# The second network's down product in units of seven products, with row sums on GpSimd

## The chip, the cores and the metric

The kernel runs on one core of a Trainium2 chip. The metric is the device time of one execution in microseconds, and the time of a kernel is the median of its runs. The engines are called PE (TensorE, with PEld for its weight loads), DVE (VectorE), ACT (ScalarE), POOL (GpSimd) and SP (SyncE, which here issues the large transfers).

## The reference, cut to what matters

Two transformer blocks follow one another on one sequence of 256 tokens of width 2048, all in float32. The second block ends with a gated network whose down product is changed here:

```python
def conv_ffn(h, w_up, conv_w, w_down):
    u = h @ w_up                                   # (256, 2048) @ (2048, 11264)
    ... causal depthwise convolution of width 3 over the tokens ...
    gate, val = jnp.split(c, 2, axis=-1)
    return (jax.nn.silu(gate) * val) @ w_down      # (256, 5632) @ (5632, 2048)

x = x + rms_norm(conv_ffn(h, ffn_w_up[i], ffn_conv[i], ffn_w_down[i]), norm_g[i, 3])
```

The norm divides each token's row by the root of its mean square and multiplies it with a gain for each column. Its result is added to the residual x and returned.

## The kernel before, in words

Every large product is done as float32 in two parts. A tile of weights, called a chunk (128 x 2 x 512 values: two blocks k of 128 rows and 512 columns), is fetched by SP into `raw`. ACT rounds it to a shorter format (`cast`, tile `whi`), DVE takes the difference to the original (`subtract`, tile `wlo`), and PE multiplies three times: high rows by high weights, high by low, low by high. The rows (the activations, transposed) are split in the same manner: `Hh` and `Hl` hold the hidden activations of the second network, 44 blocks k of 128 by 256 tokens.

A plain chunk takes two k by two halves of the tokens by three, which is 12 matmuls of 512 columns. They accumulate in two PSUM banks for each group of 512 output columns. The down product of the second network (stage `dn2`) has 4 groups of 22 chunks, 88 in all, one group after the other. Group i has the banks 2i and 2i + 1.

The order of all of this is one list, `weight_steps`. Each engine's program goes through it and does its own part of each step. ACT and DVE run up to three steps ahead of PE (`ahead`), as far as the ring of `whi` and `wlo` tiles lets them: there are three slots, and a fourth one (`WX`) in the first network. `side_steps` gives work that is put at a step; an engine does it after the casts or subtractions that are ahead of that step. `empties` does the same for finished groups. Waits are on semaphores counted in program order, so an instruction that waits also holds what stands behind it on its engine. SP fetches in the list's order and waits for a free slot of `raw`.

The first network's down product (stage `dn`) already has nine **units of seven products**. A unit takes the two chunks of one pair p of blocks k in two neighbouring groups of columns. This is a 2 x 2 by 2 x 2 block product: rows (token half by k) times columns (k by group). The Winograd form of Strassen's scheme needs seven products for it in place of eight. It needs sums of the weights, which DVE makes (`wsum`: one instruction of 1024 elements and two of 512, on tiles `RX` and `TD`), and sums of the rows, which DVE makes too (`xa`, `xc`). In the list a unit has four steps:

- `c`: two products with the original weights,
- `f`: two products with changed weights,
- `b`: one product with the sum in `TD`,
- `h`: two products with changed weights.

Plain chunks (`w`) stand between them. `stream_unit` issues the 21 matmuls. Four of the seven products (the kinds) are wanted by more than one output tile, so they have banks 4 to 7 of their own and are added to the outputs by DVE afterwards (`fold0` to `fold3`, after ACT's `fsnap` has copied one bank).

At the end of the kernel `stream_last` does the last three chunks by token half: all of them for the first 128 tokens, then for the others. For each half, ACT squares the last group straight out of PSUM, DVE makes the mean, multiplies the last group by the gain `GB` and waits for POOL, which takes the power -0.5. DVE then updates x in four instructions, and SP writes each one out.

Of the kernel before, what the change touches and what calls it, by code (L numbers as in the profile page):

```python
# [12 lines left out]
ALU = mybir.AluOpType  # L13
# [24 lines left out]
EXP = (4, 8, 12, 16, 5, 9)  # L38

# [9 lines left out]
def weight_chunks():  # L49
# [44 lines left out]
    product("dn2", "ffn_w_down_2", n4, FT)  # L94
# [36 lines left out]
def down_chunks(chunks):  # L131

    return {(row[1], row[2] // 2): t for t, row in enumerate(chunks) if row[0] == "dn"}


def down_units(chunks):

    at = down_chunks(chunks)
    return {at[2 * h + z, p]: (3 * h + q, z) for h in range(2) for q, p in enumerate(DU[h]) for z in range(2)}
# [30 lines left out]
def weight_steps(chunks):  # L170
# [21 lines left out]
    return rows + [("w", t) for t in range(IN2, END)]  # L192
# [67 lines left out]
def side_steps(chunks):  # L260
# [133 lines left out]
    for g in range(2 * NF):  # L394
        for f in range(4):
            for j in range(3 if g % 2 == 0 else 5):
                put(FF2 + 8 * g + 8 + 2 * f + j, "conv%d" % j, 4 * g + f)
    return at
# [64 lines left out]
def build(nc, A):  # L463
    ctx = ExitStack()
    with ctx:
# [86 lines left out]
        MG2 = at("MG2", rT, 0, [2, D])  # L552
        NAT = at("NAT", rN, 0, [2, 1024])
# [82 lines left out]
        forms = form_order(chunks)  # L636
        form_rank = {p: r for r, (p, _) in enumerate(forms)}
# [35 lines left out]
        def unit_steps(n):  # L673
            i, p = (0, DU[0][n]) if n < 3 else (2, DU[1][n - 3])
            return {kind: step_of[kind, down[i + (kind == "f"), p]] for kind in "cfbh"}
# [7 lines left out]
        def whole(u):  # L683

            kind, t = work[u]
            if kind == "b":
                return TD[:, units[t][0] % 2, :]
# [111 lines left out]
        def sync_program(eng):  # L799
            sp = Seat(eng)  # L800

            def fetch(t):
                _, _, k0, a, n, name, c = chunks[t]
                if t in units and raw_before[t] < DN:
                    sp.wait_ge(s_mm, upto[DN])
                elif raw_before[t] is not None:
# [40 lines left out]
        def gpsimd_program(eng):  # L847
# [11 lines left out]

            eng.memset(MHALF[:, :], -0.5).then_inc(s_mhalf, 1)  # L860
# [46 lines left out]
            row_rstd(7)  # L907
            for t in range(2):
# [4 lines left out]
        def scalar_program(eng):  # L913
# [44 lines left out]
            def empty(g):  # L958
# [73 lines left out]
                elif st in ("post", "dn2"):  # L1032
                    for t in range(2):
# [4 lines left out]
                        square(b[t][:, :], 6 if st == "post" else 8, 4 * t + i)  # L1038
# [5 lines left out]
            def side(name, i, t):  # L1044
# [128 lines left out]
                elif name == "fsnap":  # L1173
# [3 lines left out]
                    copy(SD[:, 0, :], bank[4][:, :]).then_inc(s_snap, 1)  # L1177
                elif name == "sqb":
# [97 lines left out]
        def vector_program(eng):  # L1276
# [50 lines left out]
            def empty(g):  # L1327
# [92 lines left out]
                elif st == "dn2":  # L1420
                    if i < 3:
                        ve.wait_ge(l_g3, 16)
                        for t in range(2):
                            cs_ = slice(512 * i, 512 * (i + 1))
                            ve.wait_ge(s_sq, SQ[7] + 2 * i + t + 1)
                            eng.tensor_tensor(MG2[:, t, cs_], b[t][:, :], GB[:, cs_], ALU.mult).then_inc(s_emptyV, 1)
# [62 lines left out]
            def side(name, i, t):  # L1489
# [177 lines left out]
                elif name == "wsum":  # L1667

                    h, p = (0, DU[0][i]) if i < 3 else (2, DU[1][i - 3])
                    for z in range(2):  # L1670
                        n = down[h + z, p]
# [4 lines left out]
                    ve.wait_ge(s_wsum, 3 * i + 1)  # L1676
                    if i >= 2:
# [3 lines left out]
                    eng.tensor_tensor(TD[:, i % 2, :], z[:, 3, :], z[:, 0, :], ALU.subtract).then_inc(s_wsum, 1)  # L1681
                    ve.wait_ge(s_wsum, 3 * i + 2)
                    eng.tensor_tensor(z[:, 1, :], z[:, 1, :], TD[:, i % 2, :], ALU.subtract).then_inc(s_wsum, 1)
# [17 lines left out]
                elif name == "fold3":  # L1701
# [4 lines left out]
                    eng.tensor_tensor(xs, xs, SD[:, 2, :], ALU.add).then_inc(s_fold, 1)  # L1706
                elif name == "between":
# [161 lines left out]
            b = [bank[z] for z in banks["dn2", 3]]  # L1869
            for t in range(2):  # L1870
# [5 lines left out]
                eng.tensor_tensor(MG2[:, t, 1536:D], b[t][:, :], GB[:, 1536:D], ALU.mult).then_inc(s_emptyV, 1)  # L1876
                ve.wait_ge(s_rs, 9 + t)
                for c in range(4):
                    xs = slice(512 * c, 512 * (c + 1))
                    ve.wait_ge(*emptied_at(("dn2", c), t))  # L1880
                    eng.scalar_tensor_tensor(out=X[:, t, xs], in0=MG2[:, t, xs], scalar=rs_7[:, t:t + 1],
                                             in1=X[:, t, xs], op0=ALU.mult, op1=ALU.add).then_inc(s_fin, 1)


        def tensor_program(eng):
# [35 lines left out]
            def begins(g, half):  # L1921
# [4 lines left out]
                if g[0] == "dn2":  # L1926
                    pe.wait_ge(s_cv0, 84 if g[1] < 2 else 88)
# [9 lines left out]
            def stream_unit(u):  # L1937
# [3 lines left out]
                h, k = n // 3 > 0, chunks[t][2]  # L1941
                left, right = ("dn", 2 * h), ("dn", 2 * h + 1)
                opens, ends = n in (0, 3), n in (2, NU - 1)
                hi, lo = two(hi_at(u)), two(lo_at(u))

                def rows(k, half):
                    return tuple(z[:, half * P:(half + 1) * P] for z in hidden(k))

                def sums_of_rows(z):
                    e = ex_at(n)  # L1950
# [4 lines left out]
                if kind == "c":  # L1955
                    products = ((None, 4, rows(k, 0)), (left, 0, rows(k + 1, 0)))
                elif kind == "b":
                    products = ((None, 5, sums_of_rows(2)),)
                elif kind == "f":
                    products = ((None, 6, sums_of_rows(3)), (right, 0, sums_of_rows(4)))  # L1960
# [445 lines left out]
```

## Time and profile before

| what | value |
|---|---|
| median of 3 runs | 2325.8 us (2325.62 to 2333.89) |
| span of the profiled execution | 2323.6 us, 2.2 us below the median |
| PE busy | 2303.2 us, 99% |
| VectorE busy | 1689.3 us, 73% |
| ScalarE busy | 1255.4 us, 54% |
| GpSimd busy | 20.3 us, 1% |
| moved by DMA | 439.28 MB, 189 GB/s on average |

The profile is one execution. The span goes from its first to its last instruction; the time of the same execution outside the profiler is not given beside it, so the median of the runs stands for it, and the 2.2 us between the two is what lies around the span. A busy PE need not be a PE at its peak, because matmuls overlap and their ends are modelled: the distance from one start to the next counts, not the recorded duration.

### The profile page before, as it was taken

What the parts mean: (1) busy time and instruction counts of PE and PEld (TensorE: products, weight loads), DVE (VectorE), ACT (ScalarE), POOL (GpSimd) and SP (SyncE); (2) the same over time, 40 slices, a digit from 0 to 9 for tenths busy, and PEclk for the clock granted to TensorE, in tenths of its full rate; (3) what the DMA queues carried; (4) which work ended last, traced back from release to release, by engine and by line L of the source; (5) the groups of instructions that cost most, each with busy time, mean ns of one, the idle gap of its engine ahead of it and who ended that gap; (6) DMA issues with size and microseconds to landing.
All of it is one profiled execution on the core that took longest, in us unless ns stands there. A gap on an engine that the chain in (4) does not pass through costs nothing.

```text
span 2323.6 us, 29041 instructions
## 1 busy us (share of the span) xinstructions
PE 2303.2 (99%) x11236; PEld 1941.5 (84%) x11236; DVE 1689.3 (73%) x2356; ACT 1255.4 (54%) x1854; POOL 20.3 (1%) x34
## 2 busy tenths in 40 slices
PE   9999999999999999999999999999999999999998
PEld 7888888888788888888888888888888888888887
DVE  6445565666788888887878777967888888885444
ACT  7445464555555555555655567866444444444443
POOL 1000000000000000000000000000000000000000
PEclk9999999999999999999999999999999999999999
DMA  8665555557555656556566755455666666666665
GB/s 268 194 185 171 157 175 151 186 185 239 185 178 194 215 181 204 203 172 186 189 210 204 225 179 176 140 168 179 189 189 189 190 189 191 190 190 194 193 193 162
DMA packets 226425, 439.28 MB, mean 189 GB/s; under 512 B 13632, under 2 KB 17888, under 8 KB 225904
## 3 DMA queue, kind: packets, MB, share of 16 engines
q1 hardware_dynamic: 224400, 429.51, 58.5%
q0 software_dynamic: 1888, 7.93, 1.1%
q8 instruction: 88, 1.44, 0.3%
q14 instruction: 49, 0.40, 0.0%
HBM read 435.24 MB, written 2.15 MB: 188 GB/s over the span
## 4 chain that ended last, share of the span: by engine, by line
PE 94%; DVE 3%; ACT 1%; issue 1%; DMA 0%; SPq 0%; DVEq 0%; POOLq 0%; POOL 0%; ACTq 0%
PE bank L2043 20%; PE bank L2045 20%; PE bank L2044 20%; PE bank L2093 14%; PE bank L2095 7%; PE bank L2014 2%; PE bank L2016 2%; PE bank L2015 2%; PE bank L2105 2%; DVE wlo L1314 1%; PE bank L1969 1%; PE bank L1967 1%; PE bank L1968 1%; ACT whi L950 1%; PE bank L2148 0%
## 5 line engine op out<-in xcount | busy, mean ns | idle before, releaser
L1314 DVE TENSOR_TENSOR wlo<-raw,whi 128x1024 fp32r<-128x1024 f32 (+2 forms) x683 | 829.9, 1216 | 527.6 <-ACT whi L950 525.2
L950 ACT CAST whi<-raw 128x1024 fp32r<-128x1024 f32 (+2 forms) x683 | 712.3, 1043 | 825.4 <-PE bank L2045 564.7
L2093 PE MATMUL bank<-TT,whi 128*128 128x512 f32 x1408 | 488.9, 392 | 0.8 <-DVE TT L1579 0.8
L2043 PE MATMUL bank<-whi,TT 128*128 128x512 f32 (+1 forms) x1116 | 439.8, 394 | 1.7 <-DVE wlo L1314 1.1
L2045 PE MATMUL bank<-whi,TT 128*128 128x512 f32 (+1 forms) x1116 | 433.0, 388 | 0.0
L2044 PE MATMUL bank<-wlo,TT 128*128 128x512 f32 (+1 forms) x1116 | 432.5, 388 | 0.0
L2095 PE MATMUL bank<-TT,wlo 128*128 128x256 f32 x1408 | 394.4, 280 | 0.0
L2093 PEld LDWEIGHTS bank<-TT,whi 128*128 128x128 f32 x1408 | 263.4, 187 | 58.7 <-issue 1.3
L2095 PEld LDWEIGHTS bank<-TT,wlo 128*128 128x128 f32 x1408 | 266.6, 189 | 0.0
L2043 PEld LDWEIGHTS bank<-whi,TT 128*128 128x128 f32 x1116 | 209.7, 188 | 44.0 <-DVE wlo L1314 1.5
L2045 PEld LDWEIGHTS bank<-whi,TT 128*128 128x128 f32 x1116 | 209.5, 188 | 43.2
L2044 PEld LDWEIGHTS bank<-wlo,TT 128*128 128x128 f32 x1116 | 209.9, 188 | 40.6
L950 ACT CAST whi<-PB 128x1024 fp32r<-128x1024 f32 (+1 forms) x90 | 90.7, 1008 | 84.8 <-PE bank L2045 65.0
L2045 PE MATMUL bank<-whi,Hl 128*128 128x512 f32 x340 | 132.4, 389 | 0.0
L2044 PE MATMUL bank<-wlo,Hh 128*128 128x512 f32 x340 | 132.4, 389 | 0.0
L2043 PE MATMUL bank<-whi,Hh 128*128 128x512 f32 x340 | 132.4, 389 | 0.0
L1314 DVE TENSOR_TENSOR wlo<-PB,whi 128x1024 fp32r<-128x1024 f32 (+1 forms) x90 | 104.6, 1166 | 22.5 <-ACT whi L950 21.6
L2043 PE MATMUL bank<-whi,HI 128*128 128x512 f32 x212 | 83.0, 392 | 0.0
L2045 PE MATMUL bank<-whi,HL 128*128 128x512 f32 x212 | 82.6, 390 | 0.0
L2044 PE MATMUL bank<-wlo,HI 128*128 128x512 f32 x212 | 82.6, 389 | 0.0
L2044 PEld LDWEIGHTS bank<-wlo,Hh 128*128 128x128 f32 x340 | 63.8, 188 | 13.3
L2045 PEld LDWEIGHTS bank<-whi,Hl 128*128 128x128 f32 x340 | 63.8, 188 | 13.3
(367 smaller groups left out, 3323.3 us busy)
## 6 DMA issues: line engine op xcount, KB each, us to landing
raw<-in_ffn_w_up_dram SPq DMA_DIRECT2D x176, 512.0 KB, 3.4
raw<-in_w_in_dram SPq DMA_DIRECT2D x120, 512.0 KB, 3.7
raw<-in_ffn_w_down_dram SPq DMA_DIRECT2D x88, 512.0 KB, 4.7
raw<-in_w_down_dram SPq DMA_DIRECT2D x70, 512.0 KB, 4.7
raw<-in_w_gate_dram SPq DMA_DIRECT2D x55, 512.0 KB, 3.6
raw<-in_w_up_dram SPq DMA_DIRECT2D x55, 512.0 KB, 3.8
raw<-in_swa_w_in_dram SPq DMA_DIRECT2D x48, 512.0 KB, 3.7
PB<-in_w_gate_dram SPq DMA_DIRECT2D x33, 512.0 KB, 4.8
```

The source lines that it names most:

```text
L950: eng.copy(parted(hi_at(u), src), src).then_inc(s_cast, 1)
L1314: eng.tensor_tensor(parted(lo_at(u), src), src, parted(hi_at(u), src).bitcast(F32), ALU.subtract).then_inc(s_lo, 1)
L1967: eng.matmul(o[:, :], lh, hi[:, b, :], start=g is None and opens, stop=False)
L2014: eng.matmul(o[:, :], lh, hi[:, b, :], start=fresh, stop=False, skip_group_check=chain)
L2015: eng.matmul(o[:, :], lh, lo[:, b, :], start=False, stop=False, skip_group_check=chain)
L2016: mm = eng.matmul(o[:, :], ll, hi[:, b, :], start=False, stop=read, skip_group_check=chain)
L2043: eng.matmul(o, lh[:, ts], hi[:, kk, :], start=start, stop=False, skip_group_check=chain)
L2044: eng.matmul(o, lh[:, ts], lo[:, kk, :], start=False, stop=False, skip_group_check=chain)
L2045: mm = eng.matmul(o, ll[:, ts], hi[:, kk, :], start=False, stop=stop, skip_group_check=chain)
L2093: eng.matmul(o[:, :], hi[:, kk, fs], TT[:, k, :, :].rearrange("p a s -> p (a s)"), start=k == 0, stop=False)
L2095: mm = eng.matmul(o[:, 0:S], lo[:, kk, fs], Th[:, k, :], start=False, stop=k == KT - 1)
L2105: return eng.transpose(out, src, ident[:, :])
```

## The change

All 88 chunks are still fetched. The stage `dn2` now runs in two halves of two column groups each. The first half has five units (pairs p = 0 to 4) with four plain chunks in each turn, after ten plain chunks. The second half has seven units (p = 2 to 8) with three plain chunks in each turn, after three plain chunks. Four plain chunks close the first half. In the second half two chunks of group 2 and four of group 3 close. The ring has its fourth slot here too.

The sums of the rows are made by POOL (`sums_of_rows`): for each of the nine pairs that some unit uses, it adds `Hh` and `Hl` (512 elements), makes four sums of 128 elements, waits for ACT's cast of them (`vb`) and subtracts (512 elements). Pairs 2, 3 and 4 are used by both halves from the same tiles; there are three tiles.

The kinds of the first half have banks 4 to 7, those of the second half banks 0 to 3. After the last unit of a half ACT copies the first kind into the output tile `MG2` (`vsnap`). DVE adds the others there (`vfold0` to `vfold3`), and later each group's own two banks (`sum_of`). Squares and gains then work from that tile. The last four chunks, not three, are done by token half. In the ending DVE does the sum, the gain, the mean and the four updates for each token half.

The diff, cut:

```diff
+VU = ((0, 1, 2, 3, 4), (2, 3, 4, 5, 6, 7, 8))
+VW = ((4, 4, 4, 4, 4), (3, 3, 3, 3, 3, 3, 3))
+VFIRST = (10, 3)
+VCLOSE = ((20, 20), (20, 18))
+VROWS = (0, 1, 2, 3, 4, 5, 6, 7, 8)
+VROW = (0, 1, 2, 3, 4, 2, 3, 4, 5, 6, 7, 8)
+VTILES = 3
+LAST = 4
...
+def last_steps():
+
+    rows = []
+    for h in range(2):
+        i = 2 * h
+        turn = [("w", i + z, p) for p in range(21) for z in range(2) if p not in VU[h] and p < VCLOSE[h][z]]
+        turn[1], turn[2] = turn[2], turn[1]
+        rows += turn[:VFIRST[h]]
+        turn = turn[VFIRST[h]:]
+        for p, n in zip(VU[h], VW[h]):
+            c, f, b, d = ((kind, i, p) for kind in "cfbh")
+            w, turn = turn[:n], turn[n:]
+            rows += [c] + w[:2] + [f] + w[2:3] + [b] + w[3:4] + [d] + w[4:]
+        assert not turn
+        rows += [("w", i + z, p) for z in range(2) for p in range(VCLOSE[h][z], 22)]
+    return rows
...
-        z = min(range(RING + 1 if FFN <= t < IN2 else RING), key=lambda x: used.get(x, x - 100))
+        z = min(range(RING + 1 if FFN <= t < IN2 or t >= DN2 else RING), key=lambda x: used.get(x, x - 100))
...
+    for m, r in enumerate(VROW):
+        h = m >= len(VU[0])
+        c = stands.index(num[2 * h, VROWS[r]])
+        put(stands[c - 1], "wsum", NU + m)
+        if r not in done:
+            done.add(r)
+            put(stands[c - 1], "vb", r)
+    kinds = last_steps()
+    for h in range(2):
+        over = kinds.index(("h", 2 * h, VU[h][-1]))
+        n = stands.index(num[kinds[over + 1][1:]])
+        put(stands[n], "vsnap", h)
+        for j in range(4):
+            put(stands[n], "vfold%d" % j, h)
+    for i in range(3):
+        put(stands[stands.index(num[i, 21]) + 3 - (i == 2)], "vgain", i)
...
+        VX = at("VX", rT, 1024, [2, S])
+        VS = at("VS", rT, 1536, [4, P])
+        VD = at("VD", rT, 3072, [2, 512])
+        LG = at("LG", rW, 0, [2, 512])
...
# GpSimd's program
+            def sums_of_rows(r):
+
+                k = 2 * VROWS[r]
+                po.wait_ge(s_H2, k + 2)
+                eng.tensor_tensor(VX[:, :, :], Hh[:, k:k + 2, :].bitcast(F32), Hl[:, k:k + 2, :].bitcast(F32),
+                                  ALU.add).then_inc(s_xs, 1)
+                a11, a21, a12, a22 = (VX[:, z // 2, (z % 2) * P:(z % 2 + 1) * P] for z in range(4))
+                s1, s2, s3, s4 = (VS[:, z, :] for z in range(4))
+                po.wait_ge(s_xs, XS0 + r + 1)
+                eng.tensor_tensor(s1, a21, a22, ALU.add).then_inc(s_xsum, 1)
+                eng.tensor_tensor(s3, a11, a21, ALU.subtract).then_inc(s_xsum, 1)
+                po.wait_ge(s_xsum, XSUM0 + 4 * r + 1)
+                eng.tensor_tensor(s2, s1, a11, ALU.subtract).then_inc(s_xsum, 1)
+                po.wait_ge(s_xsum, XSUM0 + 4 * r + 3)
+                eng.tensor_tensor(s4, a12, s2, ALU.subtract).then_inc(s_xsum, 1)
+                po.wait_ge(s_exhi, EX0 + r + 1)
+                hi, lo = rows_of(r)
+                eng.tensor_tensor(lo, VS[:, :, :], hi.bitcast(F32), ALU.subtract).then_inc(s_ex, 1)
...
+            po.wait_ge(s_mm, upto[DN2])
+            for r in range(len(VROWS)):
+                sums_of_rows(r)
# ScalarE's program
+                elif name == "vb":
+                    ac.wait_ge(s_xsum, XSUM0 + 4 * i + 4)
+                    if i >= VTILES:
+                        ac.wait_ge(*rows_free(i - VTILES))
+                    elif i:
+                        ac.wait_ge(s_H2, FT)
+                    copy(rows_of(i)[0], VS[:, :, :]).then_inc(s_exhi, 1)
+                elif name == "vsnap":
+                    ac.wait_ge(s_mm, unit_steps((NU + len(VU[0]), len(table))[i] - 1)["h"] + 1)
+                    copy(merged(0, 2 * i), bank[4 - 4 * i][:, :]).then_inc(s_snap, 1)
...
# VectorE's program
+            def sum_of(i, t):
+
+                g = ("dn2", i)
+                if t == 0:
+                    ve.wait_ge(s_half, main_no[g] + 1)
+                else:
+                    ve.wait_ge(s_mm, upto[last[g] + 1])
+                ve.wait_ge(s_snap, SNAP0 + i // 2 + 1)
+                ve.wait_ge(s_fold, FOLD0 + 4 * (i // 2) + 4)
+                m = merged(t, i)
+                eng.tensor_tensor(m, bank[banks[g][t]][:, :], m, ALU.add).then_inc(s_emptyV, 1)
...
+                elif name == "vfold0":
+
+                    ve.wait_ge(s_snap, SNAP0 + i + 1)
+                    eng.tensor_tensor(merged(0, 2 * i + 1), bank[5 - 4 * i][:, :], merged(0, 2 * i),
+                                      ALU.add).then_inc(s_fold, 1)
...
+            for t in range(2):
+                sum_of(3, t)
+                last_gain(t)
+                ending(t)
                 for c in range(4):
...
+                    output(t, c)
# PE's program
-                if g[0] == "dn2":
-                    pe.wait_ge(s_cv0, 84 if g[1] < 2 else 88)
+                if g[0] == "dn2" and g[1] < 2:
+                    pe.wait_ge(s_cv0, 84)
+                elif g == ("dn2", 2) and half == 0:
+                    pe.wait_ge(s_snap, SNAP0 + 1)
+                elif g[0] == "dn2":
+                    pe.wait_ge(s_fold, FOLD0 + (1 if g[1] == 2 else (2, 4)[half]))
...
-                if t >= END - RING:
+                if t >= END - LAST:
```

In the ending, `last_gain` multiplies the last group by the gain into the tile `LG`, `ending` is the mean of one token half, and `output` is one update of x.

## Rows read from the trace of the kernel before

**Rows 1.** The page: busy time of each engine, granted clock in 40 slices.

```profile
PE 2303.2 (99%) x11236; PEld 1941.5 (84%) x11236; DVE 1689.3 (73%) x2356; ACT 1255.4 (54%) x1854; POOL 20.3 (1%) x34
...
PEclk9999999999999999999999999999999999999999
```

**Rows 2.** Groups by line from 2040 us on: xcount | busy, mean ns | idle.

```profile
L2045 PE MATMUL bank<-whi,Hl 128*128 128x512 f32 x340 | 132.4, 389 | 0.0
...
L2061 PE MATMUL bank<-whi,Hh 128*128 128x512 f32 x12 | 4.7, 390 | 0.0
```

**Rows 3.** ScalarE's timeline in the changed stage: start, duration, instruction, idle before.

```profile
2297.00 1.05 ACT L950 CAST whi<-raw 128x1024 fp32r<-128x1024 f32 x1 [1.67 <-PE bank L2045]
2299.72 1.05 ACT L950 CAST whi<-raw 128x1024 fp32r<-128x1024 f32 x1 [1.67 <-PE bank L2045]
```

**Rows 4.** Stretches: length, busy us of PE, PEld, DVE, ACT, POOL, PEclk, DMA.

```profile
1210.00:1283.00 73.00, 73.00 (x324) 60.25 (x323) 60.37 (x67) 39.52 (x43) 0.60 (x1) 1.00 0.58 193
2110.00:2307.00 197.00, 197.00 (x871) 163.18 (x870) 92.59 (x79) 79.65 (x85) 0.00 (x0) 1.00 0.62 190
```

**Rows 5.** Timeline of the end, ScalarE, VectorE and GpSimd.

```profile
2316.03 0.60 ACT L926 ACTIVATE JK<-bank 128x512 bf16<-128x512 f32 x1 [3.40 <-PE bank L2063]
...
2317.01 0.68 DVE L1876 TENSOR_TENSOR MG<-bank,GB 128x512 f32<-128x512 f32 x1
2317.17 0.55 POOL L910 TENSOR_TENSOR RS<-MEAN,MHALF 128x1 f32<-128x1 f32 x1 [3.54 <-DVE MEAN L1875]
2317.76 2.74 DVE L1881 SCALAR_TENSOR_TENSOR X<-MG,RS,X 128x512 f32<-128x512 f32 x4
```

**Rows 6.** Groups by line in the first network's down product.

```profile
L1675 DVE TENSOR_TENSOR RX<-RX 128x1024 f32<-128x1024 f32 x9 | 11.0, 1218 | 0.0
...
L1681 DVE TENSOR_TENSOR TD<-RX 128x512 f32<-128x512 f32 x9 | 6.2, 692 | 0.3
...
L1314 DVE TENSOR_TENSOR wlo<-TD,whi 128x512 fp32r<-128x512 f32 x6 | 4.1, 684 | 0.0
...
L950 ACT CAST whi<-TD 128x512 fp32r<-128x512 f32 x6 | 3.7, 618 | 1.1 <-PE bank L2045 0.8 <-PE bank L1969 0.3
```

**Rows 7.** Timeline of one unit there, VectorE, then PE.

```profile
1255.53 1.22 DVE L1675 TENSOR_TENSOR RX<-RX 128x1024 f32<-128x1024 f32 x1
...
1258.12 1.22 DVE L1314 TENSOR_TENSOR wlo<-raw,whi 128x1024 fp32r<-128x1024 f32 x1
...
1260.76 0.39 PE L2043 MATMUL bank<-whi,HI 128*128 128x512 f32 x1
```

**Rows 8.** Timeline of an earlier unit, VectorE, then PE.

```profile
1234.88 0.68 DVE L1640 TENSOR_TENSOR XR<-HI,HL 128x512 f32<-128x512 f32 x1
...
1238.26 1.23 DVE L1314 TENSOR_TENSOR WX<-raw,WX 128x1024 fp32r<-128x1024 f32 x1 [1.04 <-ACT WX L950]
...
1239.54 0.50 PE L2043 MATMUL bank<-WX,HI 128*128 128x512 f32 x1
1239.88 0.39 PE L2044 MATMUL bank<-WX,HI 128*128 128x512 f32 x1
```

**Rows 9.** Timeline of GpSimd's powers and of VectorE beside them.

```profile
44.93 0.72 POOL L854 TENSOR_TENSOR RS<-MEAN,MHALF 128x2 f32<-128x2 f32 x1 [10.93 <-DVE MEAN L1434]
...
45.35 1.23 DVE L1314 TENSOR_TENSOR wlo<-raw,whi 128x1024 fp32r<-128x1024 f32 x1 [0.50 <-ACT whi L950]
...
54.69 1.22 DVE L1314 TENSOR_TENSOR wlo<-raw,whi 128x1024 fp32r<-128x1024 f32 x1
...
54.93 1.53 POOL L854 TENSOR_TENSOR RS<-MEAN,MHALF 128x2 f32<-128x2 f32 x1 [5.31 <-DVE MEAN L1434]
...
55.83 0.28 DVE L1294 TENSOR_TENSOR RA<-NAT,CS 128x128 f32<-128x128 f32 x1
```

**Rows 10.** Timeline of GpSimd at the start.

```profile
0.73 0.10 POOL L860 MEMSET MHALF<- 128x2 f32 x1 [0.29 <-POOLq L2390]
...
6.38 0.31 POOL L872 MEMSET KR<- 64x256 f32 x1
```

More of the change, by code:

```diff
@@ L93, in weight_chunks @@
         product("val2", "ffn_w_up_2", vals, KT, 0, [f])
-    product("dn2", "ffn_w_down_2", n4, FT)
+    for kind, i, p in last_steps():
+        for j in ((i,) if kind == "w" else (i, i + 1) if kind == "c" else ()):
+            rows.append(("dn2", j, 2 * p, 2, 512, "ffn_w_down_2", 512 * j))
     assert len(rows) == END
@@ L191, in weight_steps @@
     rows += [(kind, down[i + (kind == "f"), p]) for kind, i, p in down_steps()]
-    return rows + [("w", t) for t in range(IN2, END)]
+    rows += [("w", t) for t in range(IN2, DN2)]
+    down = down_chunks(chunks, "dn2")
+    return rows + [(kind, down[i + (kind == "f"), p]) for kind, i, p in last_steps()]
 def ring_slots(work):
@@ L636, in build @@
         forms = form_order(chunks)
+        table = unit_table()
+        down_at = {st: down_chunks(chunks, st) for st in ("dn", "dn2")}
         form_rank = {p: r for r, (p, _) in enumerate(forms)}
@@ L686, in whole @@
             if kind == "b":
-                return TD[:, units[t][0] % 2, :]
+                return (TD if t < DN2 else VD)[:, units[t][0] % 2, :]
             if kind == "H":
@@ L805, in fetch @@
                     sp.wait_ge(s_mm, upto[DN])
+                elif t in units and t >= DN2 and raw_before[t] < DN2:
+                    sp.wait_ge(s_mm, upto[DN2])
                 elif raw_before[t] is not None:
@@ L1419, in empty, with gain_of @@
                         eng.tensor_tensor(o, b[t][:, :], o, ALU.add).then_inc(s_emptyV, 1)
[L1420 to L1426, printed above, removed]
+                elif st == "dn2" and i < 3:
+                    for t in range(2):
+                        sum_of(i, t)
+            def sum_of(i, t):
[8 more added lines that the diff above has]
+                eng.tensor_tensor(m, bank[banks[g][t]][:, :], m, ALU.add).then_inc(s_emptyV, 1)
+            def gain_of(i, t):
+                m = merged(t, i)
+                ve.wait_ge(l_g3, 16)
+                ve.wait_ge(s_sq, SQ[7] + 2 * i + t + 1)
+                eng.tensor_tensor(m, m, GB[:, 512 * i:512 * (i + 1)], ALU.mult).then_inc(s_mg, 1)
             def mean_of(r):
@@ L1867, in vector_program, with ending @@
                         side(name, i, t)
-            b = [bank[z] for z in banks["dn2", 3]]
-            for t in range(2):
+            def ending(t):
                 m = MEAN[:, 8, t:t + 1]
@@ L1940, in stream_unit @@
                 n = units[t][0]
-                h, k = n // 3 > 0, chunks[t][2]
-                left, right = ("dn", 2 * h), ("dn", 2 * h + 1)
-                opens, ends = n in (0, 3), n in (2, NU - 1)
+                st, i, p = table[n]
+                k, b0 = 2 * p, 0 if (st, i) == ("dn2", 2) else 4
+                left, right = (st, i), (st, i + 1)
+                opens, ends = p == (DU if st == "dn" else VU)[i // 2][0], p == (DU if st == "dn" else VU)[i // 2][-1]
                 hi, lo = two(hi_at(u)), two(lo_at(u))
                 def rows(k, half):
-                    return tuple(z[:, half * P:(half + 1) * P] for z in hidden(k))
+                    parts = hidden(k) if st == "dn" else operand(st, k)
+                    return tuple(z[:, half * P:(half + 1) * P] for z in parts)
                 def sums_of_rows(z):
+                    if st == "dn2":
+                        r = VROW[n - NU]
+                        pe.wait_ge(s_ex, EX0 + r + 1)
+                        return tuple(y[:, z - 1, :] for y in rows_of(r))
                     e = ex_at(n)
```

91 lines of the change are left out of this document (67 added, 24 removed).

## The prediction

> **What bounds the kernel now.** I read the engine table first: PE is busy for 2303.2 of 2323.6 us, with the granted clock in every slice in the top tenth, its 2.4 GHz level [rows 1]. The reader should see that only fewer matmuls, or a matmul that starts too late, can move the time much. The grouped view of the stretch from 2040 us on gives the product that is changed: three lines with 340 matmuls of 512 columns each, and three with 12 at the end, 1056 in all, which is 88 chunks of 12 [rows 2]. Their recorded 389 ns overlap, so the pitch is taken elsewhere: ScalarE's casts there are released by PE, one for each chunk, at 2297.00 and 2299.72, and 2.72 us for 12 matmuls is 0.227 us for one [rows 3]. In that stretch VectorE is busy for 92.6 of 197 us and ScalarE for 79.7 [rows 4]; GpSimd does nothing. The first network's down product already runs nine units of seven products; there PE is busy for 73 of 73 us while VectorE is at 60.4 [rows 4]. The chain's end belongs to the second half of the tokens: square, mean, GpSimd's power, four updates on VectorE, transfer [rows 5].
>
> **Part 1, matmuls.** A unit takes 21 matmuls where two chunks took 24. Twelve units save 36, and 36 x 0.227 = 8.2 us, all on the path, since PE is never idle there.
>
> **Part 2, weights.** A unit casts and subtracts 3.5 chunks instead of 2: 1.05 + 0.62 us more on ScalarE [rows 3, 6], 1.22 + 0.68 more on VectorE, and the three weight sums 1.22 + 0.69 + 0.69 = 2.6 us on VectorE [rows 6]. Twelve units make 20 us on ScalarE and 54 on VectorE. Row casts and snapshots (11 x 0.62) and VectorE's folds and sums out of PSUM (16 new instructions at 0.68 [rows 5], 10.9 us) come on top: VectorE goes from 93 to about 158 us in a stretch of 190, 83%. That is off the path on average; what matters is the turn of a unit. In the diff's second half it has three plain chunks: PE needs 4.76 + 8.16 = 12.9 us; VectorE, one 1024-wide subtraction starting some 1.14 us after the other when it is pressed, 6 x 1.14 + 0.61 + 2.6 = 10.1. The first half's turn has four plain chunks: 15.6 against 11.2. The first network's second half has just the former turn.
>
> There I read the lead of the steps. The tight one is the second plain chunk, whose subtraction stands behind the weight sums: it ends at 1258.12 + 1.22 = 1259.34 and PE takes the chunk up at 1260.76, a lead of 1.4 us [rows 7]. Where VectorE had row work in the turn as well (1.7 us from 1234.88 on), a later chunk's lead was gone: subtraction until 1239.49, matmul at 1239.54, the next one 0.34 instead of 0.23 us behind it [rows 8]. That cost PE 0.12 us. So the weights alone stay hidden behind PE.
>
> **Part 3, the row sums on GpSimd.** Nine rows, each of two instructions of 512 elements and four of 128, with two inputs, beside VectorE's subtractions. ScalarE's row cast at a unit's beginning sets them off, so they fall into the tight place: the subtraction that ends one row, then the additions of the next. As operands they are needed about 8 us later (PE has the unit's first product and two plain chunks before) and one unit later, which covers their own length. What they do to VectorE the trace does not show, so it is bounded. From below: GpSimd's small powers delay no VectorE instruction. The subtraction at 45.35 begins inside the power at 44.93 and takes 1.23 us as always, and the product at 55.83 keeps its 0.28 us inside the power that lasts until 56.46 [rows 9]. That gives 0. From above: GpSimd itself is held. A power of this form takes 0.72 us, but 1.53 at 54.93, when a VectorE subtraction with two SBUF inputs was running until 55.91 [rows 9]. If this works the other way round for an instruction's whole length, the length counts. Nearest rows: a memset of 256 elements takes 0.31 and one of 2 elements 0.10, 0.81 ns for an element of one stream [rows 10]; two input streams make 0.83 us for 512 elements. The fixed part is 0.38: the power takes 0.55 for one element [rows 5] and 0.72 for two, 0.17 for each. That is 1.21 us for 512 elements and 0.59 for 128. Before the tight chunk stand two long and two short ones, 3.6 us against a lead of 1.4: a stall of 2.2 us in each of the eight units that both finish a row and begin the next (five in the first half, three in the second), 17.6 in all. The ends are 0 and 17.6. I take 1.0 us, eight times the 0.12 of [rows 8], because the rows nearest to the question show VectorE undelayed. This is the weakest choice of the sum: those powers read two elements and the sums read 512.
>
> That 1.53 against 0.72 [rows 9] shows an exclusion in one direction. The Trainium skill (SBUF — State Buffer, section SBUF: two separate sides) says that the shared port pair is an exclusive lock, held for the whole instruction by whoever starts first, and that a VectorE instruction with two SBUF inputs takes part. By that rule the upper end would stand in the sum and not the lower; the row agrees for GpSimd as the one that waits, and nothing here shows VectorE waiting.
>
> **Part 4, borders.** Folds and snapshot between the halves run while PE has the four closing chunks, 10.9 us. From the last unit's end: a cast 1.05, the snapshot 0.62, a subtraction 1.22 and four folds of 0.68, 5.6 us; nothing is late, and if it were, it would cost what it is late. SyncE fetches the same 88 tiles and waits in its queue for the units' slots, as in the first network, where PE did not wait. GpSimd begins row 0 ten chunks (27 us) ahead of its unit, beside the convolution's last groups; its length is covered, and the most that it can cost there is the 3.6 us less a lead as in [rows 7], once. Value taken: 0.
>
> **Part 5, the ending.** Four chunks by token half instead of three: the second half of the tokens takes PE 24 x 0.227 = 5.44 us instead of 4.08. Before the square now stands the sum out of PSUM, 0.68 us and some 0.07 for the handover; the gain goes beside the square. The chain from square to last update takes 2317.76 + 2.74 - 2316.03 = 4.5 us [rows 5], and 5.2 with the sum, less than 5.44, so the first half's chain does not hold up the second's. Plus 0.75 us.
>
> **Sum.** -8.2 + 1.0 + 0.75 = -6.4 us: the span goes from 2323.6 to 2317.2. The median of the runs shown, 2325.8, is 2.2 above that span, and I carry the 2.2: 2319.4 us.
>
> **Rivals.**
> (a) GpSimd holds VectorE, and the kernel is slower than before. Place: VectorE's queue between a unit's first and second plain chunk. For it: the 1.53, and that up to six row instructions fall into VectorE's closest packed stretch [rows 7]. Against it: no VectorE instruction of this trace is lengthened. Price: 8 x 2.2 = 17.6 us, or 8 x 1.3 = 10 if half of the fixed parts does not hold the engine (4 x 0.19 less, and a little lead regained). With -8.2 + 0.75 that is +2.5 to +10 us, 2328 to 2336. It decides from 7.45 us of stall on, 0.93 us for each of the eight units.
> (b) VectorE is held only while elements stream: 2 x 0.83 + 2 x 0.21 = 2.1 us, 0.7 over the lead, 5.6 in all: -1.9 us, 2324; with part of the lead regained 2321. For and against it the same rows.
> (c) The saving is not reached: a border's bank or a unit's tile comes late. For it: twelve units, nearly twice as dense in the first half as in the first network's. Against it: that product ran without a wait. 2321 to 2330.
> (d) Row work costs nothing at all: -7.4 us, 2318.4; counted with the forecast.
>
> **Chances.** Forecast with (d) 0.47, its own range 2317.5 to 2321; (b) 0.2; (a) 0.28; (c) 0.05. The range of 80%, 2317 to 2332, takes in the forecast, (b), (c) and the lower half of (a). Half a percent, 11.6 us, is about what a measurement of this kernel can tell from no change. Faster than 2314.2 needs more than the 8.2 us that there are: 0.03. Slower than 2337.4 needs (a) above its upper price: 0.07. Within half a percent: 0.9.
>
> **What would show it.** PE: 1020 matmuls in this product at the same pitch. GpSimd: row instructions near 1.2 and 0.6 us where VectorE rests. For (a): subtractions or weight sums on VectorE longer than 1.23 and 0.69 us, or gaps between them while GpSimd works, and PE waiting for lower parts in units with a row but not in units 5 to 7, which have none. For the forecast: VectorE's durations unchanged, PE's waits in the stretch under 2 us. The ending: 5.2 instead of 4.5 us from the last matmul to the last update. A PE wait at the first chunk of columns 1024 on would speak for (c). Wrong altogether: a pitch that changes, or fewer than 36 matmuls gone.

## The result and the profile after

The changed kernel takes 2338.8 us (median of five runs, 2337.1 to 2339.4) against 2325.8 before: 13.0 us more, a ratio of 1.0049 with an interval of 1.0034 to 1.0065. The forecast was 2319.4 with a range up to 2332. The sign was wrong and the time lies outside the range. The change is small, but its interval lies wholly above 1. About one execution in five of the kernel before takes some 9 us more than the others at the same granted clock (2333.9 among 2325.2 to 2326.1 here), which the medians pass over and which widens the intervals.

The page of the kernel after, its head and the engine table:

```profile
span 2336.0 us, 29186 instructions
...
PE 2302.0 (99%) x11200; PEld 1936.1 (83%) x11200; DVE 1773.7 (76%) x2432; ACT 1280.0 (55%) x1889; POOL 93.3 (4%) x88
```

The 36 matmuls are gone (11236 before [rows 1]), yet the span is 12.4 us longer. PE's busy share still says 99%; that hides the loss. The waits of PE from 2070 us on show it (the line that waits, what released it: us in total, times, longest). The kernel before has no such line in this product:

```profile
PE bank L2223 <- DVE wlo L1430: 7.9, 4, 2.5
PE bank L2223 <- DVE WX L1430: 5.3, 6, 1.2
```

So PE waits for the lower parts of the weights, which VectorE makes, and always at line 2223, the first product of a plain chunk. Here are the windows (columns as in [rows 4]) of the stage, and of two pieces after one of these waits:

```profile
2110.00:2290.00 180.00, 167.99 (x713) 135.62 (x711) 146.02 (x126) 87.10 (x98) 59.73 (x43) 0.97 0.55 182
2250.00:2255.00 5.00, 5.00 (x18) 3.98 (x18) 3.77 (x4) 0.62 (x1) 1.25 (x1) 0.75 0.63 206
2255.00:2260.00 5.00, 5.00 (x24) 4.14 (x23) 2.41 (x3) 2.63 (x3) 0.22 (x1) 1.00 0.01 3
```

PE is idle for 12 of 180 us, and its clock is 0.97 of full on average: 0.75 in one piece, full in the next. VectorE's row shows the cause. Its timeline in the second half's fourth unit, where one row is finished and the next begun:

```profile
2243.49 2.10 DVE L1806 TENSOR_TENSOR RX<-RX 128x1024 f32<-128x1024 f32 x1
2245.62 1.67 DVE L1815 TENSOR_TENSOR VD<-RX 128x512 f32<-128x512 f32 x1
2247.32 0.83 DVE L1817 TENSOR_TENSOR RX<-RX,VD 128x512 f32<-128x512 f32 x1
2248.07 1.47 DVE L1430 TENSOR_TENSOR wlo<-raw,whi 128x1024 fp32r<-128x1024 f32 x1
2249.47 1.47 DVE L1430 TENSOR_TENSOR WX<-raw,WX 128x1024 fp32r<-128x1024 f32 x1
```

GpSimd beside it:

```profile
2242.70 1.80 POOL L957 TENSOR_TENSOR EXL<-VS,EXH 128x512 fp32r<-128x512 f32 x1 [66.17 <-ACT EXH L1019]
2244.47 2.27 POOL L944 TENSOR_TENSOR VX<-Hh,Hl 128x512 f32<-128x512 f32 x1
2246.82 0.78 POOL L949 TENSOR_TENSOR VS<-VX 128x128 f32<-128x128 f32 x1
2247.56 0.90 POOL L950 TENSOR_TENSOR VS<-VX 128x128 f32<-128x128 f32 x1
2248.42 1.43 POOL L952 TENSOR_TENSOR VS<-VS,VX 128x128 f32<-128x128 f32 x1
```

And PE:

```profile
2246.68 0.39 PE L2149 MATMUL bank<-whi,Hl 128*128 128x512 f32 x1
2249.60 0.79 PE L2223 MATMUL bank<-whi,Hh 128*128 128x512 f32 x1 [2.52 <-DVE wlo L1430]
2250.19 0.63 PE L2224 MATMUL bank<-wlo,Hh 128*128 128x512 f32 x1
2250.61 0.63 PE L2225 MATMUL bank<-whi,Hl 128*128 128x512 f32 x1
...
2252.32 0.49 PE L2223 MATMUL bank<-whi,Hh 128*128 128x512 f32 x1
2252.65 0.40 PE L2224 MATMUL bank<-wlo,Hh 128*128 128x512 f32 x1
```

The three weight sums took 1.22, 0.69 and 0.69 us before [rows 6]; here 2.10, 1.67 and 0.83. The subtraction behind them takes 1.47 instead of 1.22. The engines take turns: the first sum begins at 2243.49 inside GpSimd's 1.80, which ends near 2244.5, and ends itself at 2245.6, 1.1 us after that, where it takes 1.22 alone; GpSimd's next begins at 2244.47, needs 1.3 alone (below), and ends at 2246.7. Up to the end of that subtraction VectorE has lost 6.07 - 3.83 = 2.24 us. The matmul at 2249.60 starts 2.92 us after the last one instead of 0.23. Then the matmuls start 0.43 us apart: the granted clock is 0.50 of full from 2249.6 to 2252.3, the 1.2 GHz level. The eight steps to 2252.65 take 3.05 us instead of 1.81. This one stall cost 2.7 + 1.2 = 3.9 us.

A unit of the second half without row work (2219 us), where I expected no wait, has one too. VectorE:

```profile
2216.50 1.23 DVE L1806 TENSOR_TENSOR RX<-RX 128x1024 f32<-128x1024 f32 x1
2217.76 0.69 DVE L1815 TENSOR_TENSOR VD<-RX 128x512 f32<-128x512 f32 x1
2218.48 0.69 DVE L1817 TENSOR_TENSOR RX<-RX,VD 128x512 f32<-128x512 f32 x1
```

and PE:

```profile
2219.70 0.39 PE L2149 MATMUL bank<-WX,Hl 128*128 128x512 f32 x1
2220.37 0.50 PE L2223 MATMUL bank<-whi,Hh 128*128 128x512 f32 x1 [0.28 <-DVE wlo L1430]
2220.70 0.40 PE L2224 MATMUL bank<-wlo,Hh 128*128 128x512 f32 x1
```

Here nothing is drawn out, and still 0.55 us are lost (0.67 - 0.23, and 0.11 at the next step). This 0.44 and VectorE's 2.24 above make up the 2.7 of the long stall. The waits of the stage fall into four kinds:

| units | what comes late | lost in each, us | sum, us |
|---|---|---|---|
| first half, 2nd to 5th | second plain chunk | 1.13 + 0.11 | 5.0 |
| second half, 2nd and 3rd (no row work) | first plain chunk | 0.44 + 0.11 | 1.1 |
| second half, 4th to 6th (one row finished, one begun) | first plain chunk | 2.69 + 1.24 | 11.8 |
| second half, 7th (one row finished) | first plain chunk | 1.31 + 0.11 | 1.4 |

They make 19.3 us together, and 2323.6 - 8.2 + 0.8 (the ending) + 19.3 = 2335.5, against a span of 2336.0. Without any wait the span would be 2316.2. The median is 2.8 us above the profiled span, where the forecast carried 2.2.

The first unit of the first half does not stand in the table, and it tells something. There GpSimd finishes one row and begins the next too, and VectorE's three sums are drawn out as much (2.31, 1.67 and 0.84 us from 2102.89 on). But the subtraction of the unit's second plain chunk had ended before them, at 2102.98, and PE took that chunk up at 2107.22 without a wait.

The ending, VectorE and GpSimd (the last matmul starts at 2327.26):

```profile
2327.68 0.69 DVE L1550 TENSOR_TENSOR MG<-bank,MG 128x512 f32<-128x512 f32 x1 [0.20 <-PE bank L2243]
...
2329.59 0.56 POOL L1012 TENSOR_TENSOR RS<-MEAN,MHALF 128x1 f32<-128x1 f32 x1 [4.88 <-DVE MEAN L2029]
2330.18 2.08 DVE L2042 SCALAR_TENSOR_TENSOR X<-MG,RS,X 128x512 f32<-128x512 f32 x3 [0.68 <-POOL RS L1012]
2332.18 0.75 DVE L2042 SCALAR_TENSOR_TENSOR X<-LG,RS,X 128x512 f32<-128x512 f32 x1
```

From the sum to the end of the last update it takes 5.25 us, where the chain from the square took 4.47 [rows 5].

### The profile page after: what moved, and what is told of

It is laid out like the page before. It is cut to its first block, busy times and chain, and to the rows that moved or that the text cites. A ratio compares the mean times of both kernels' runs of the same rounds, so it can differ in the third digit from the quotient of the medians.

```text
span 2336.0 us, 29186 instructions
## 1 busy us (share of the span) xinstructions
PE 2302.0 (99%) x11200; PEld 1936.1 (83%) x11200; DVE 1773.7 (76%) x2432; ACT 1280.0 (55%) x1889; POOL 93.3 (4%) x88
## 4 chain that ended last, share of the span: by engine, by line
PE 90%; DVE 6%; ACT 2%; issue 1%; DMA 0%; SPq 0%; DVEq 0%; POOLq 0%; POOL 0%; ACTq 0%
PE bank L2223 19%; PE bank L2225 19%; PE bank L2224 19%; PE bank L2273 14%; PE bank L2275 7%; PE bank L2194 2%; PE bank L2196 2%; PE bank L2195 2%; PE bank L2285 2%; DVE wlo L1430 2%; PE bank L2149 1%; PE bank L2148 1%; PE bank L2147 1%; ACT whi L1052 1%; DVE RX L1806 1%
## 5 line engine op out<-in xcount | busy, mean ns | idle before, releaser
L1430 DVE TENSOR_TENSOR wlo<-raw,whi 128x1024 fp32r<-128x1024 f32 (+2 forms) x638 | 776.8, 1219 | 419.6 <-ACT whi L1052 416.8
L1052 ACT CAST whi<-raw 128x1024 fp32r<-128x1024 f32 (+2 forms) x638 | 664.8, 1043 | 711.3 <-PE bank L2225 451.1
L1052 ACT CAST WX<-raw 128x1024 fp32r<-128x1024 f32 x65 | 68.3, 1050 | 65.8 <-PE bank L2225 61.8
L1430 DVE TENSOR_TENSOR WX<-raw,WX 128x1024 fp32r<-128x1024 f32 x65 | 80.6, 1241 | 27.3 <-ACT WX L1052 26.8
L1430 DVE TENSOR_TENSOR wlo<-RX,whi 128x1024 fp32r<-128x1024 f32 x51 | 64.0, 1257 | 28.6 <-ACT whi L1052 26.9
L1052 ACT CAST whi<-RX 128x1024 fp32r<-128x1024 f32 x51 | 53.5, 1050 | 46.6 <-PE bank L2225 27.2
L2223 PE MATMUL bank<-whi,Hh 128*128 128x512 f32 x160 | 64.7, 404 | 7.9 <-DVE wlo L1430 7.9
```

Source lines behind the costliest of these rows:

```text
L1052: eng.copy(parted(hi_at(u), src), src).then_inc(s_cast, 1)
L1430: eng.tensor_tensor(parted(lo_at(u), src), src, parted(hi_at(u), src).bitcast(F32), ALU.subtract).then_inc(s_lo, 1)
L2223: eng.matmul(o, lh[:, ts], hi[:, kk, :], start=start, stop=False, skip_group_check=chain)
```

## The experiments

Two theories were set against each other. L: VectorE and GpSimd exclude one another for a whole instruction, and VectorE is held at the tight place. O: the order of a unit's steps in the second half has taken VectorE's lead away, whoever makes the rows. Both can be true at once. The times are medians of 6 to 12 executions, but for one run that is named, and the ratios are to the kernel before.

**Three rows for all twelve units.** GpSimd makes three rows only. The kernel uses them again for every unit, so the sums belong to other rows than the reference's, and six rows' sums are left out; all other work stays.

```
-VROWS = (0, 1, 2, 3, 4, 5, 6, 7, 8)
-VROW = (0, 1, 2, 3, 4, 2, 3, 4, 5, 6, 7, 8)
+VROWS = (0, 1, 2)
+VROW = (0, 1, 2, 0, 1, 2, 0, 1, 2, 0, 1, 2)
...
-        c = stands.index(num[2 * h, VROWS[r]])
+        c = stands.index(num[2 * h, VU[h][m - h * len(VU[0])]])
```

The last two lines keep each unit's weight sums at their place.

> The changed kernel with the sums of three rows only, all made by GpSimd before the fourth unit; the other units multiply with those three rows' sums again (the output leaves the other six rows' sums out). Same matmuls, same casts and weight sums, same turns. Theory L (GpSimd's row instructions hold VectorE back in the tight place of the turn): the stalls of the units with row work from the fourth on go. Of the 20.5 us that PE lost in the changed kernel some 5 stay (two stalls of 1.24 us in the first half, about 0.55 in each later unit of the second half, which two units without row work showed); time 2323 to 2325, VectorE's weight sums back at 1.22 and 0.69 us from the fourth unit on. Theory W (the units stand too densely for VectorE, whatever GpSimd does): PE still waits 2 to 3 us in the late units, the clock still falls, time 2333 or more.

Measured: 2322.6 us, ratio 0.9982 (0.9971 to 0.9992), span 2321.2. PE's waits:

```profile
PE bank L2223 <- DVE WX L1430: 1.5, 3, 1.0
PE bank L2223 <- DVE wlo L1430: 1.1, 4, 0.3
```

One wait of 1.0 is left in the first half (where a row is still made) and six of 0.2 to 0.3 in the second. 1.24 + 6 x 0.55 = 4.5, and 2316.2 + 4.5 = 2320.7. VectorE's weight sums take 1.22 and 0.69 us again from the fourth unit on. The row work beyond the third row cost 14.8 us by the spans and by the waits (19.3 - 4.5), 16.2 by the medians. L holds. Theory W of the expectation, that the units are too dense whatever GpSimd does, fails: PE has no long wait left. The time is a little under the expected 2323, with one stall in the first half where two were expected. What is left in the second half has nothing to do with rows: O holds as well, for a smaller part.

**The turn as in the first network.** In the second half step b is put directly behind f, ahead of the third plain chunk. In the changed kernel it stood behind that chunk:

```
-            rows += [c] + w[:2] + [f] + w[2:3] + [b] + w[3:4] + [d] + w[4:]
+            rows += [c] + w[:2] + [f] + (w[2:3] + [b] + w[3:4] if n > 3 else [b] + w[2:3]) + [d] + w[4:]
```

> The changed kernel with the steps b and third plain chunk of the second half's turn exchanged, which is the order of the first network's units. Nothing else. Theory O (in the changed kernel's turn the weight sums stand in front of the first plain chunk's subtraction, with less lead than in the first network's): the two stalls of 0.55 us in units without row work go, and the three of some 4.3 us, clock included, fall to about the 1.24 of the first half, the last one of 1.4 goes: 2325.5 to 2328. Rival (the order does not matter, only the sum of VectorE's and GpSimd's work in a turn does): 2337 to 2339.

Measured: 2326.9, ratio 1.0011 (0.9994 to 1.0029), span 2325.0. PE in a unit of the second half:

```profile
2248.54 0.39 PE L2225 MATMUL bank<-whi,Hl 128*128 128x512 f32 x1
2249.89 0.50 PE L2223 MATMUL bank<-WX,Hh 128*128 128x512 f32 x1 [0.96 <-DVE WX L1430]
2250.23 0.39 PE L2224 MATMUL bank<-WX,Hh 128*128 128x512 f32 x1
```

Seven waits are left, the first half's four and three of the second half (its 4th to 6th unit), all alike: a step of 1.35, then 0.34, and then 0.23 again. The clock did not fall. 7 x 1.24 = 8.7, and 2316.2 + 8.7 = 2324.9. The turn was worth 10.6 of the 19.3 us: the 0.55 in each unit, and in the units with rows what the tighter place added, three falls of the clock (3.7 us) among it.

**The turn, and the rows later.** In addition ScalarE's row cast, which sets GpSimd off, moves from the chunk ahead of a unit to the chunk behind its first step:

```
-            put(stands[c - 1], "vb", r)
+            put(stands[c + 1], "vb", r)
```

> As the run before, and ScalarE's row cast, which sets GpSimd off, stands two chunks later in every unit, where VectorE has over 2 us of lead. GpSimd does the same instructions. Theory L with O: nothing stalls any more or under 0.3 us a unit, the clock stays: the full -8.2 + 0.8, 2318 to 2320.5. Rival (GpSimd's holding costs VectorE 2.3 us a unit wherever it stands, and the turn of 12.9 us has no room for it): stalls of 1 to 2 us stay in the units with rows, 2326 or more. A second danger: the last row instruction comes too late for step f, then PE waits at f.

Measured: 2317.8, ratio 0.9962 (0.9947 to 0.9976), span 2315.8; PE has no wait in the stretch. The stage's window:

```profile
2110.00:2290.00 180.00, 180.00 (x795) 148.80 (x794) 158.39 (x138) 98.04 (x110) 62.74 (x48) 1.00 0.59 193
```

VectorE:

```profile
2255.11 2.31 DVE L1430 TENSOR_TENSOR WX<-RX,WX 128x1024 fp32r<-128x1024 f32 x1
2257.34 1.77 DVE L1430 TENSOR_TENSOR wlo<-VD,whi 128x512 fp32r<-128x512 f32 x1
...
2264.66 1.21 DVE L1806 TENSOR_TENSOR RX<-RX 128x1024 f32<-128x1024 f32 x1
```

VectorE is held as much as before (2.31 for a 1.22, 1.77 for a 0.68; busy for 1771.2 us in the whole run against 1773.7 in the changed kernel), but where it has a lead; the weight sums have their old length. The time is 0.2 us under the expected 2318. So it was the place, not the amount, and the whole 8.2 us come out: 2323.6 - 8.2 + 0.8 = 2316.2 against 2315.8.

**Rows later, with the changed kernel's own turn.** Only the second of these two edits.

> The changed kernel with its own turn, only ScalarE's row cast two chunks later. Theory: the two causes are separate and both are needed. GpSimd's part goes (no weight sum longer than 1.22 us), the turn's own stall stays in the second half: six or seven times 0.55 us, as with three rows only. 2316.2 span by the matmuls and the ending, plus 3.3 to 3.9: time 2321 to 2323. Rival (the later cast alone is enough): 2318. Rival (in this turn the later place meets the first plain chunk as well): 2328 or more.

Measured: 2322.3, ratio 0.9991 (0.9978 to 1.0004), span 2320.4. There is no wait in the first half. In the second there are three of 0.55 and three of 0.83 us each, 4.1 in all, and 2316.2 + 4.1 = 2320.3. The longer three, which the expectation did not have, are those of the units that follow a unit with row work. No weight sum is drawn out. Neither edit alone does it: the turn alone leaves 8.7 us of the stalls, the later rows alone 4.1.

**GpSimd's sums beside the kernel before.** Eight rows' sums are made by GpSimd into tiles that nothing reads; the product stays at twelve matmuls a chunk. This was executed once only.

```
+            for r in range(8):
+                po.wait_ge(s_mm, upto[DN2 + 26 + 6 * r])
+                ...
+                eng.tensor_tensor(VX[:, :, :], Hh[:, 2 * r:2 * r + 2, :].bitcast(F32), Hl[:, 2 * r:2 * r + 2, :].bitcast(F32),
+                                  ALU.add).then_inc(s_xs, 1)
```

> The kernel before with eight rows' sums made by GpSimd beside its down product, into a scratch tile that nobody reads, so only the contention is new. VectorE has half of its time free there. Theory L (the pair is exclusive, held by the one that has it): subtractions that meet a row instruction are started late or last up to 1.0 us longer (1.4 to 2.3 instead of 1.22), row instructions that meet a subtraction last longer in turn, and the time stays within 1 us of before. Rival (VectorE was lengthened in the changed kernel by something else, such as ScalarE or the tiles' places): all subtractions keep 1.22 us.

Measured: 2324.9, span 2323.1, no wait of PE. It gives GpSimd's bare lengths, and shows the exclusion with nothing else changed. GpSimd:

```profile
2146.98 1.29 POOL L917 TENSOR_TENSOR VX<-Hh,Hl 128x512 f32<-128x512 f32 x1 [545.53 <-PE bank L2068]
2148.35 1.33 POOL L922 TENSOR_TENSOR VS<-VX 128x128 f32<-128x128 f32 x1
2149.64 0.47 POOL L923 TENSOR_TENSOR VS<-VX 128x128 f32<-128x128 f32 x1
```

VectorE:

```profile
2145.29 1.23 DVE L1337 TENSOR_TENSOR wlo<-raw,whi 128x1024 fp32r<-128x1024 f32 x1 [1.49 <-ACT whi L973]
2148.01 1.34 DVE L1337 TENSOR_TENSOR wlo<-raw,whi 128x1024 fp32r<-128x1024 f32 x1 [1.50 <-ACT whi L973]
2150.73 1.41 DVE L1337 TENSOR_TENSOR wlo<-raw,whi 128x1024 fp32r<-128x1024 f32 x1 [1.37 <-ACT whi L973]
```

The subtraction at 2148.01 starts inside GpSimd's first addition (until 2148.27), is 0.11 us longer than its 1.23, and then holds the 0.47 us addition of 128 elements back to 1.33. Whoever comes second waits until the other's instruction ends, less some 0.15 us (here 0.11 of the 0.26 that were left, in the changed kernel 0.87 of 1.01 at 2243.49), and the record counts that wait as its own duration. The subtractions lose 0.2 us at most here, and not the up to 1.0 of the expectation: it is mostly GpSimd that comes second. With idle time behind every subtraction this costs nothing.

**The rows by VectorE itself.** With the turn as in the first network, VectorE makes the sums between its subtractions, and GpSimd none.

```
-            put(stands[c - 1], "vb", r)
+            put(stands[c - 3], "va", r)
+            put(stands[c - 2], "vb", r)
+            put(stands[c], "vc", r)
...
```

Not shown is `sums_of_rows`, which moves from GpSimd's program into VectorE's steps `va` (the additions) and `vc` (the subtraction).

> First network's order of the turn, and the row sums made by VectorE itself (1 addition, 4 small ones, 1 subtraction, 2.2 us a row) in the part of the turn where it has lead; GpSimd does nothing. If GpSimd's use is worth its price: VectorE would need 12.3 of 12.9 us in units with a row, and PE waits 0.1 to 0.6 us in each of the eight: 2319 to 2323. If it is worth nothing (VectorE has the room): 2317.5 to 2318.5, like GpSimd with the later cast.

Measured: 2317.9, ratio 0.9960 (0.9945 to 0.9975), span 2315.5, no wait of PE. VectorE's row instructions:

```profile
2255.66 0.69 DVE L1842 TENSOR_TENSOR EXL<-VS,EXH 128x512 fp32r<-128x512 f32 x1
...
2256.86 0.69 DVE L1828 TENSOR_TENSOR VX<-Hh,Hl 128x512 f32<-128x512 f32 x1
2257.58 0.29 DVE L1833 TENSOR_TENSOR VS<-VX 128x128 f32<-128x128 f32 x1
```

A row costs VectorE 2 x 0.69 + 4 x 0.29 = 2.5 us. In the 180 us window it is busy for 153.9 us with all rows, and for 158.4 with the rows given to GpSimd. The offload relieved it of less than the holding put on it. The times of the two are the same (2317.8 and 2317.9).

**Three closing chunks by token half instead of four**, on the version without waits.

```
-LAST = 4
+LAST = 3
```

> The fastest version so far (first network's order, later row cast) with the last three chunks by token half, as before the change, and not four. The first half's chain of 5.2 us is then longer than PE's 4.08 us of the second half and holds VectorE: 1.1 us later at the end, 2318.9 if that version takes 2317.8. Rival (the chain's updates fit in anyway): no difference, under 0.3 us.

Measured: 2319.0, ratio 0.9969 (0.9956 to 0.9981), 1.2 us above that version. VectorE:

```profile
2307.48 0.74 DVE L2042 SCALAR_TENSOR_TENSOR X<-LG,RS,X 128x512 f32<-128x512 f32 x1
2308.14 0.68 DVE L1550 TENSOR_TENSOR MG<-bank,MG 128x512 f32<-128x512 f32 x1
```

The last matmul starts at 2306.64, the sum out of PSUM only at 2308.14, 1.5 us later, behind the first token half's last update. With four chunks it starts 0.4 us behind the last matmul. The 1.2 us rest on medians whose intervals overlap. The 1.1 of the trace are the firmer number, though the two spans differ by 0.6 only (2316.4 and 2315.8), because in this execution the last matmul starts 0.5 us earlier.

**Thirteen units**, a sixth in the first half: three matmuls fewer. The version is the one without waits; the tables of the rows grow by a tenth pair.

```
-VU = ((0, 1, 2, 3, 4), (2, 3, 4, 5, 6, 7, 8))
-VW = ((4, 4, 4, 4, 4), (3, 3, 3, 3, 3, 3, 3))
+VU = ((0, 1, 2, 3, 4, 5), (3, 4, 5, 6, 7, 8, 9))
+VW = ((3, 3, 3, 3, 3, 3), (3, 3, 3, 3, 3, 3, 3))
...
```

> The fastest version with thirteen units, six in the first half with three plain chunks in each turn, in the first network's order. Three matmuls fewer, -0.68 us: 2317.1. Rival (the first half's turn of 12.9 us is too dense, with a row in every unit and VectorE at about 13.5 us with what GpSimd holds): 0.3 to 1 us more in each of its units, 2318.5 to 2322.

Measured with the rows on GpSimd: 2318.6, ratio 0.9963 (0.9948 to 0.9977), span 2316.0. It is not faster than twelve units: in four first-half units the third plain chunk, behind b, starts 0.33 to 0.43 us after the matmul before it and the next step takes 0.34. That is 0.2 to 0.3 us lost in each, some 1.1 us together, and more than the 0.7 us saved. The forecast of a gain was a miss, and its rival held: with the rows on GpSimd this turn is too dense, as VectorE is busy, its waits for GpSimd counted in, for 69.3 of the 70 us from 2110 on.

> Thirteen units as in the run before last, six in the first half, and VectorE makes the row sums. GpSimd's holding costs VectorE some 3.4 us a row, its own instructions 2.2, and the waits of 0.2 to 0.3 us before the first half's units with GpSimd's rows were small: they go, and the three matmuls fewer count. 0.68 us below the version with twelve units and VectorE's rows: 2317.2. Rival (VectorE at 12.3 of 12.9 us in six turns in a row falls behind): waits of 0.1 to 0.5 us a unit, 2318 to 2320.

Measured with the rows on VectorE: 2317.2, ratio 0.9961 (0.9948 to 0.9974), span 2314.5. This is the expected time and the lowest median of all. VectorE is busy for 64.1 of the 70 us from 2110 on, and PE has no wait. Its span is 1.0 us below that of twelve units, somewhat more than three matmuls' 0.7. Each of its six times is below each of the six with twelve units, but by little, and the kernel before was 0.2 us faster beside it as well; so a gain of some 0.7 us is likely and not shown.

## Why the prediction was wrong

- **Matmuls (part 1): right.** 36 fewer; the whole 8.2 us appear as soon as the waits are gone (2315.8 and 2315.5).
- **Weights (part 2): hidden as forecast, but not in the diff's own turn.** The forecast was 158 of 190 us of VectorE without the rows. In the version with the rows by VectorE it is busy for 162.5 of the 190 us from 2110 on, of which rows are 20, so 143 without them, and PE does not wait. The 158 was on the high side: it had twelve units where eleven lie in that window, and lengths that overlap by 0.08 us each. But the step "The first network's second half has just the former turn" was false. There b stands directly behind f; in the diff a plain chunk stands between them. The weight sums are tied to the unit's first step, and in the longer order they come ahead of the first plain chunk's subtraction. The lead of 1.4 us [rows 7] was taken from a place that this turn does not have. Alone this costs 0.55 us a unit; with the rows on top it made the stalls of 2.7 us.
- **Row sums (part 3): the choice of 1.0 us failed; this is the largest error of the sum.** In the changed kernel the rows cost 16.0 of the 19.3 us (19.3 less 6 x 0.55), and still 8.7 with the first network's order, which alone eats up the gain: -8.2 + 0.8 + 8.7 = +1.3. I took a value near the lower end because GpSimd's powers had delayed no VectorE instruction [rows 9]. Those read two elements. The other row of the same group, a power held from 0.72 to 1.53, was the one that told of the exclusion, and it works in both directions. The estimates of length were near: 1.21 and 0.59 us against 1.29 and 0.47 measured alone. The rule cited there (the Trainium skill, SBUF — State Buffer, section SBUF: two separate sides) would have put the upper end into the sum, and the trace agrees: 2.10 for 1.22 us. As cited it is about two SBUF inputs only: an instruction with an input from PSUM, below, kept its length.
- **The size of rival (a).** Its mechanism was the cause, its place ("between a unit's first and second plain chunk") right for the first half: 1.24 us in four units, not 2.2 in five. The first of the five units had its second plain chunk subtracted before the sums, as shown above. In the others VectorE lost 2.5 us up to the end of the tight subtraction (6.3 for 3.8), where the prediction counted the row instructions' whole 3.6; less the lead of 1.4 that leaves 1.1, the measured wait. In the second half the place was one chunk earlier and the price 3.9 in three units. In all PE lost 19.3 us against an upper price of 17.6. That the two are near is partly luck: the first half cost less than priced, and the false turn and the clock, which the price did not have, made up for it.
- **The clock: left out.** No term had it. Three stalls of 2.7 us cost another 1.2 us each in slow matmuls, 3.7 us together. Without them the time would be some 2335.1 us, still above the range.
- **Borders (part 4): right.** No wait at a fold, a snapshot or a bank.
- **Ending (part 5): right.** 0.78 us against 0.75. Its reason for four chunks also holds: with three, the first half's chain holds the second's up by 1.1 us.
- **The range.** It reached to the lower half of (a) as if (a) were the only fault. Two faults lay in the same place and cost more together than apart: with the better turn the rows cost 8.7, with three rows only the turn cost 3.3 (six times 0.55), and both 19.3, of which 3.7 is the clock.

## What to carry to other kernels

Work given to GpSimd was not free for VectorE when both read SBUF with two inputs: count each of its instructions as time that VectorE may lose, and put it where VectorE has a lead over PE, or leave the work on VectorE, which did it here in 0.5 to 0.6 of the time. When a turn of steps is said to be like an earlier one, write both orders out and compare them step by step with what is tied to which step. A gap of PE must be priced with what the clock does behind it: here 1.2 us for each gap of 2.5.

## What the runs showed of the hardware

The exclusion depends on where operands lie. At the first row's additions, VectorE in the changed kernel:

```profile
2076.12 1.60 DVE L1979 SCALAR_TENSOR_TENSOR C<-U,CW,C 128x256 f32<-128x256 f32 x1
2077.64 1.48 DVE L1430 TENSOR_TENSOR wlo<-raw,whi 128x1024 fp32r<-128x1024 f32 x1
2079.05 0.41 DVE L1962 TENSOR_TENSOR C<-bank,C 128x256 f32<-128x256 f32 x1
```

GpSimd beside them:

```profile
2076.14 1.30 POOL L944 TENSOR_TENSOR VX<-Hh,Hl 128x512 f32<-128x512 f32 x1 [474.69 <-PE bank L2275]
2077.52 0.52 POOL L949 TENSOR_TENSOR VS<-VX 128x128 f32<-128x128 f32 x1
2078.00 1.44 POOL L950 TENSOR_TENSOR VS<-VX 128x128 f32<-128x128 f32 x1
2079.41 0.46 POOL L952 TENSOR_TENSOR VS<-VS,VX 128x128 f32<-128x128 f32 x1
```

The update with two SBUF inputs, 0.48 us elsewhere, takes 1.60 beside the 1.30 of GpSimd. The product whose one input is a PSUM bank takes its 0.41 us while GpSimd's third instruction runs until 2079.44, and GpSimd's 0.46 us addition, which starts at 2079.41 while that product's last 0.05 us run, is not drawn out either.

GpSimd needs 1.29 us for 512 elements a partition and 0.47 for 128 when alone; VectorE needs 0.69 and 0.29 for the same. Spans of GpSimd are rough in this profile, but starts tell the same: its first addition starts 1.37 us before its second.

The clock: PE's waits in the stage are 0.3 to 1.2 us long at seven places and 2.5 at three. After the short ones the granted clock stayed at the 2.4 GHz level; after each of the long ones it was at the 1.2 GHz level for some 3 us (the matmuls' starts 0.43 us apart from 2249.60 to 2252.32).
